# Prompt attention of a decoder step: two heads at once on the two halves of TensorE, and a rearranged opening

## The reference, cut to what matters

```python
s = einsum('bkgqd,bknd->bkgqn', qi, k_cmp) - slopes * d_c      # 32 compressed blocks
p_c = where(ok_c, softmax(where(ok_c, s, NEG_INF)), 0.0)
s = einsum('bkgqd,bkqsd->bkgqs', qi, kg) - slopes * d_s        # selected blocks: at 512 tokens all of them
p_s = softmax(where(d_s >= 0, s, NEG_INF))
s = einsum('bkgqd,bskd->bkgqs', qi, kw) - slopes * d_w         # window, 512 wide: all earlier tokens
p_w = softmax(where(ok_w, s, NEG_INF))
return gi[..., 0:1] * o_c + gi[..., 1:2] * o_s + gi[..., 2:3] * o_w
```

## Time and profile before

| what | value |
|---|---|
| median of 3 runs | 3051.97 us (3050.62 to 3070.57) |
| the profiled execution's own time | 3049.01 us |
| its span | 3047.4 us |
| PE busy, PEld busy | 2885.9 us (95%), 2580.9 us (85%) |
| DVE, ACT, POOL busy | 1246.3 us (41%), 793.8 us (26%), 174.6 us (6%) |
| granted TensorE clock, mean | 0.947 |

### The profile page before, as it was taken

How to read it: one execution, slowest core, us unless ns; L and a number is a source line. 1 busy time by engine, 2 the same in 40 slices (tenths; PEclk the granted TensorE clock), 3 DMA queues, 4 the chain that set the end, 5 groups by cost and what they waited for, 6 DMA issues and landing times. The chain is left out here.

```text
span 3047.4 us, 56435 instructions
## 1 busy us (share of the span) xinstructions
PE 2885.9 (95%) x24825; PEld 2580.9 (85%) x24825; DVE 1246.3 (41%) x1997; ACT 793.8 (26%) x1382; POOL 174.6 (6%) x176
## 2 busy tenths in 40 slices
PE   6999979997999899999998989999999999999997
PEld 6999966777999547999997659999976667999997
DVE  4333355275333342433342023333546663433335
ACT  3222212232222101321220023212326652322222
POOL 1000000001111200000003000000023100000000
PEclk9999989999998558999998999999989997999999
DMA  5222210110000001322226312222221000222222
GB/s 213 93 84 85 76 62 15 69 62 24 4 3 3 32 28 46 134 82 98 83 69 167 126 52 93 76 95 82 96 94 60 1 1 15 86 95 75 94 78 72
DMA packets 36517, 214.80 MB, mean 70 GB/s; under 512 B 5200, under 2 KB 5328, under 8 KB 20336
## 3 DMA queue, kind: packets, MB, share of 16 engines
q1 hardware_dynamic: 27648, 174.34, 16.3%
q0 software_dynamic: 8720, 38.27, 4.2%
HBM read 202.49 MB, written 12.17 MB: 70 GB/s over the span
## 5 line engine op out<-in xcount | busy, mean ns | idle before, releaser
L484 PE MATMUL banks<-xh,wh 128*128 128x272 f32 x3072 | 638.9, 289 | 41.4 <-DVE wl L1435 29.0
L484 PE MATMUL banks<-xh,wl 128*128 128x272 f32 x3072 | 637.5, 289 | 0.0
L484 PE MATMUL banks<-xl,wh 128*128 128x272 f32 x3072 | 635.3, 288 | 0.0
L484 PEld LDWEIGHTS banks<-xh,wh 128*128 128x128 f32 x3072 | 485.7, 189 | 42.2 <-issue 36.4
L484 PEld LDWEIGHTS banks<-xl,wh 128*128 128x128 f32 x3072 | 484.9, 189 | 0.0
L484 PEld LDWEIGHTS banks<-xh,wl 128*128 128x128 f32 x3072 | 481.5, 190 | 0.0
L1435 DVE TENSOR_TENSOR wl<-raw,wh 128x2048 fp32r<-128x2048 f32 (+2 forms) x160 | 323.8, 2024 | 105.7 <-ACT wh L1095 105.7
L1095 ACT ACTIVATE wh<-raw 128x2048 fp32r<-128x2048 f32 (+2 forms) x160 | 270.5, 1691 | 257.9 <-PE banks L484 243.9
L484 PE MATMUL banks<-hh,wl 128*128 128x272 f32 x1408 | 291.4, 288 | 0.0
L484 PE MATMUL banks<-hh,wh 128*128 128x272 f32 x1408 | 291.1, 288 | 0.0
L484 PE MATMUL banks<-hl,wh 128*128 128x272 f32 x1408 | 290.3, 288 | 0.0
(11 more groups left out here) (292 smaller groups left out, 3135.1 us busy)
## 6 DMA issues: line engine op xcount, KB each, us to landing
raw<-in_w_in SPq DMA_DIRECT2D x88, 1024.0 KB, 4.8
raw<-in_w_out SPq DMA_DIRECT2D x32, 768.0 KB, 4.2
raw<-in_w_out SPq DMA_DIRECT2D x32, 640.0 KB, 3.8
raw<-in_w_rk SPq DMA_DIRECT2D x8, 1024.0 KB, 4.8
arena<-in_pages_c POOLq DMA_DIRECT2D x32, 256.0 KB, 7.4
raw<-in_w_kv SPq DMA_DIRECT2D x6, 1024.0 KB, 5.0
raw<-in_w_v SPq DMA_DIRECT2D x4, 1024.0 KB, 4.8
raw<-in_w_o SPq DMA_DIRECT2D x4, 1024.0 KB, 4.8
```

What stands on the lines that cost most here:

```text
L484: ins = mm(pst[:, bank + half, 0:HALF], wt[:, s, w], a[:, half * HALF:(half + 1) * HALF], start=first, stop=last)
```

## The change

Attention works in 32 steps S of a pair of heads (`i = S // 4`, both `p`) and one query tile (`qt = S % 4`).

- `scores(S, k)` does the selected (k = 0) and window keys (k = 1) for both heads, on row halves 0 to 63 and 64 to 127 of the array, into banks 2p+k. The compressed scores of both are one K = 128 product with `kbd`, a block-diagonal copy of the compressed keys (64 columns, bank 4).
- `values(S)` does one query tile for both heads, alternating the two column halves of the array (output rows 0 to 63 and 64 to 127 of bank 5).
- Turned blocks form groups that alternate banks 6 and 7: for qt 0 and 1 one group of both branches for each head, for qt 2 and 3 two groups for each head, and last one for the compressed block of both: 3 or 5 groups a step. `turns_to(S)` counts the groups ahead of step S. Group n waits until group n-2 has been copied.
- The score buffers are six, three steps deep. The maxima, sums and factors of a step lie in `stats`, so reciprocal, gate product and negation are one instruction a step each. The slope goes into the fused instruction as a scalar; q is scaled by 1/(8 slope) instead, through `cbias`. GpSimd's 16 bias instructions go. `kbd` and `vcmp_p` take three more ScalarE copies in the key/value stage.
- GpSimd loads one sample page a step, after `fac_ready` of that step, the sample gates after step 16, and the window values `vwin_c` after the last.
- `raw[:, 1]` serves as a score buffer, so SP loads the first weights of slot 1 of `bo` only when the groups ahead of step 30 have been turned.
- Opening: `x` in four parts; `params` ahead of `const`, with its own semaphore; ScalarE does all `high` first, with the split of the first slot after the fourth, and the squares after; VectorE in the same way; GpSimd holds the LoRA weights and window copies back until both weight slots have landed twice. Only the norm's sum and what follows wait for `const`.

The core of the diff, in its added lines with context (what they replace stands in the kernel above):

```diff
+            for part in range(4):
+                sp.dma_start(hT[:, 2 * part:2 * part + 2], I["x"][:, 2 * part:2 * part + 2])\
+                    .then_inc(x_in[part], 16)
...
+            stream_split("bo", I["w_bo"], free=lambda: sp.wait_ge(turned, turns_to(PAIRS - 2)))
...
+            def scores(S, k):
+                i, qt = S // 4, S % 4
                 nk = P * (qt + 1)
+                if S:
+                    pe.wait_ge(score_taken, 6 * (S - 1) + 2 * (k + 1))
+                for p in range(2):
+                    f = slice(64 * p, 64 * p + 64)
+                    last = mm(pst[:, 2 * p + k, 0:nk], qT[f, i, qt * P:(qt + 1) * P],
+                              (kslc, kwin)[k][f, i // 4, 0:nk], start=True, stop=True)
+                last.then_inc(score_mm, 1)
...
+            def turn_group(n, blocks):
+                if n >= 2:
+                    pe.wait_ge(turn_taken, n - 1)
...
+            def turn_probs(S, p):
+                qt, n = S % 4, turns_to(S)
+                s = sbuf[(2 * S + p) % 6]
+                pe.wait_ge(p_ready, 2 * S + p + 1)
+                slc = [(s[:, x * P:(x + 1) * P], P) for x in range(qt + 1)]
+                win = [(s[:, 512 + x * P:512 + (x + 1) * P], P) for x in range(qt + 1)]
+                if qt < 2:
+                    turn_group(n + p, slc + win)
                 else:
+                    turn_group(n + 2 * p, slc)
+                    turn_group(n + 2 * p + 1, win)
...
+            def values(S):
+                i, qt = S // 4, S % 4
+                pe.wait_ge(turn_taken, turns_to(S + 1))
+                if qt == 0 and i:
+                    pe.wait_ge(o_taken, i)
+                pt = ptS[S % 2]
+                c = [slice((2 * (i // 4) + p) * 64, (2 * (i // 4) + p) * 64 + 64) for p in range(2)]
+                out = [pst[64 * p:64 * p + 64, 5, qt * P:(qt + 1) * P] for p in range(2)]
+                mm(out[0], vcmp_p[0:32, c[0]], ptc[0:32, S % 2, :], start=True, stop=False, skip_group_check=True)
                 for n, v in enumerate((v_slc, v_win)):
+                    for x in range(qt + 1):
+                        for p in (1, 0):
+                            mm(out[p], v[:, x, c[p]], pt[p][:, 512 * n + P * x:512 * n + P * x + P],
+                               start=(p == 1 and n == 0 and x == 0), stop=(p == 0 and n == 1 and x == qt),
+                               skip_group_check=True)
+                mm(out[1], vcmp_p[32:64, c[1]], ptc[32:64, S % 2, :], start=False, stop=True, skip_group_check=True)\
                     .then_inc(o_mm, 1)
...
+            for S in range(PAIRS + 4):
+                live, turning = S < PAIRS, 3 <= S < PAIRS + 3
+                if turning:
+                    turn_probs(S - 3, 0)
+                if live:
+                    scores(S, 0)
+                if turning:
+                    turn_probs(S - 3, 1)
+                if live:
+                    scores(S, 1)
+                    scores_cmp(S)
+                if turning:
+                    turn_cmp(S - 3)
+                if S == PAIRS:
                     sample_scores(0)
+                if S >= 4:
+                    values(S - 4)
...
+            act.wait_ge(params_in, 16)
+            act.wait_ge(eps_set, 3)
             for ft in range(DT):
+                if ft % 2 == 0:
+                    act.wait_ge(x_in[ft // 2], 16)
+                high(Q_G00, ft, xh)
+                if ft == 3:
+                    split("inA0", 0, 0)
+            for ft in range(DT):
                 act.wait_ge(acc_step, ft)
                 act.activation(sg[:, ft % 2, :], hT[:, ft, :], ACT.Square).then_inc(sq_done, 1)
+            act.wait_ge(const_in, 16)
...
+            def exps(S):
+                nk, x = P * (S % 4 + 1), S % 3
+                act.wait_ge(negmax, S + 1)
+                for p in range(2):
+                    s = sbuf[(2 * S + p) % 6]
+                    for n, ap in enumerate((cmpb[:, x, 32 * p:32 * p + 32], s[:, 0:nk], s[:, 512:512 + nk])):
+                        ins = act.activation(ap, ap, ACT.Exp, bias=stats[:, x, 1, 3 * p + n:3 * p + n + 1],
+                                             accum_out=stats[:, x, 2, 3 * p + n:3 * p + n + 1])
+                ins.then_inc(exp_done, 1)
+            def copies(S):
+                qt, n, pt = S % 4, turns_to(S), ptS[S % 2]
+                nk = P * (qt + 1)
+                if S >= 2:
+                    act.wait_ge(o_mm, S - 1)
+                for p in range(2):
+                    if qt < 2:
+                        act.wait_ge(turned, n + 1)
+                        act.activation(pt[p].rearrange("p (k c) -> p k c", k=2)[:, :, 0:nk],
+                                       pst[:, 6 + n % 2, 0:2 * nk].rearrange("p (k c) -> p k c", k=2), ACT.Copy)\
+                            .then_inc(turn_taken, 1)
+                        n += 1
+                    else:
+                        for k in range(2):
+                            act.wait_ge(turned, n + 1)
+                            act.activation(pt[p][:, 512 * k:512 * k + nk], pst[:, 6 + n % 2, 0:nk], ACT.Copy)\
+                                .then_inc(turn_taken, 1)
+                            n += 1
+                act.wait_ge(turned, n + 1)
+                act.activation(ptc[:, S % 2, :], pst[0:64, 6 + n % 2, 0:P], ACT.Copy).then_inc(turn_taken, 1)
+            for S in range(PAIRS + 3):
+                if S >= 3:
+                    copies(S - 3)
+                if S < PAIRS:
+                    exps(S)
...
+            dve.wait_ge(params_in, 16)
             dve.memset(eps[:, 0:1], RMS_EPS).then_inc(eps_set, 1)
             dve.memset(eps[:, 1:2], GN_EPS).then_inc(eps_set, 1)
+            dve.memset(kbd[:], 0.0).then_inc(eps_set, 1)
             clear(0)
             do(dve.tensor_scalar(const[:, C_PAR + 21 * 8:C_PAR + 22 * 8],
                                  const[:, C_PAR + Q_KA * 8:C_PAR + Q_KA * 8 + 8], -1.0, 1.0, ALU.mult, ALU.add))
             for ft in range(DT):
                 low(0, Q_G00, ft, xh, xl)
+                if ft == 3:
+                    split("inA0", 0, 0)
+            for ft in range(DT):
                 sum_square(0, ft, ft % 2)
+            dve.wait_ge(const_in, 16)
...
+            def maxes(S, k):
+                i, qt, x = S // 4, S % 4, S % 3
                 nk = P * (qt + 1)
+                dve.wait_ge(score_mm, 3 * S + k + 1)
+                if k == 0 and S >= 3:
+                    dve.wait_ge(turned, turns_to(S - 2))
+                for p in range(2):
+                    s = sbuf[(2 * S + p) % 6]
+                    n, out, src, t = ((1, s[:, 0:nk], pst[:, 2 * p, 0:nk], (3 - qt) * P),
+                                      (2, s[:, 512:512 + nk], pst[:, 2 * p + 1, 0:nk], (3 - qt) * P),
+                                      (0, cmpb[:, x, 32 * p:32 * p + 32], pst[:, 4, 32 * p:32 * p + 32],
+                                       512 + qt * NCMP))[k]
+                    w = NCMP if k == 2 else nk
+                    dve.tensor_tensor_reduce(out, src, att[:, t:t + w], SLOPES[head_of(i, p)], -3e38, ALU.add,
+                                             ALU.max, stats[:, x, 0, 3 * p + n:3 * p + n + 1])\
+                       .then_inc(score_taken, 1)
+            def negate(S):
+                dve.wait_ge(score_taken, 6 * S + 6)
+                dve.tensor_scalar(stats[:, S % 3, 1, :], stats[:, S % 3, 0, :], -1.0, None, ALU.mult)\
+                   .then_inc(negmax, 1)
+            def factors(S):
+                i, qt, x = S // 4, S % 4, S % 3
+                gates = g_p[:, qt, :].rearrange("q (k g c) -> q k g c", k=4, g=4)[:, 2 * (i // 4):2 * (i // 4) + 2, i % 4, :]
+                dve.wait_ge(exp_done, S + 1)
+                do(dve.reciprocal(stats[:, x, 3, :], stats[:, x, 2, :]))
                 own.wait()
+                fac = stats[:, x, 4, :].rearrange("q (p c) -> q p c", p=2)
+                dve.tensor_tensor(fac, stats[:, x, 3, :].rearrange("q (p c) -> q p c", p=2), gates, ALU.mult)\
+                   .then_inc(fac_ready, 1)
+                dve.wait_ge(fac_ready, S + 1)
+                c = cmpb[:, x, :].rearrange("q (p c) -> q p c", p=2)
+                for p in range(2):
+                    s, nk = sbuf[(2 * S + p) % 6], P * (qt + 1)
+                    for n, w in ((1, slice(0, nk)), (2, slice(512, 512 + nk))):
+                        ins = dve.tensor_scalar(s[:, w], s[:, w], stats[:, x, 4, 3 * p + n:3 * p + n + 1], None,
+                                                ALU.mult)
+                    ins.then_inc(p_ready, 1)
+                dve.tensor_tensor(c, c, fac[:, :, 0:1].to_broadcast([P, 2, NCMP]), ALU.mult).then_inc(cmp_ready, 1)
+            def take_out(i):
+                dve.wait_ge(o_mm, 4 * (i + 1))
+                dve.tensor_copy(oT[:, i, 0:SEQ], pst[:, 5, :]).then_inc(o_taken, 1)
+            for S in range(PAIRS + 1):
+                if S >= 8 and S % 4 == 0:
+                    take_out(S // 4 - 2)
```

(24 more changed lines are left out.)

310 lines of the change are left out of this document (91 added, 219 removed).

## The result

| | before | after |
|---|---|---|
| median, same chip | 3059.93 us (4 runs) | 3092.07 us (3088.53 to 3114.99, 4 runs) |
| the profiled execution | 3049.01 us, span 3047.4 | 3092.99 us, span 3091.3 |
| mean granted clock | 0.947 | 0.919 |

The ratio on record, taken over the executions of both kernels, is 1.0134, 95% interval 1.0093 to 1.0175: slower by 1.3%. The two medians by themselves stand 32 us apart, a ratio of 1.0105, also inside the interval; the fourth execution of the kernel before, 3067.89 us, had moved its median from 3051.97 to 3059.93. First the page of the changed kernel: busy time by engine, the clock in 40 slices of 77 us, and the chain that ended last.

What follows compares the result with a forecast made beforehand. TensorE was taken to bound nearly the whole run before, a chain through the queues attention after. 3049.0 + 39.9 (attention) + 5 (tail) - 10.5 (opening) + 0.7 (copies) = 3084, median 3 us above: 3087 us, range 3058 to 3110.

Steps and rivals of the forecast that it cites:

- The line: Prompt attention: exponentials, first copies, turns, maxima, factors and negation form one chain with nothing beside it, 35.6 us a pair at full clock.
- D: Attention: delay from the end of exps(S-1) until turn_cmp(S-3) is seen, 8.5 us a pair at full clock.
- Its terms: Attention chain, a pair: exponentials 11.1 us, VectorE 15.4, hand-overs 0.6, delay 8.5 at full clock.
- the mixed case: Attention: qt 1 at the low clock, qt 2 at the full, 37.3 us a pair; chance 0.50.
- The clock: Attention: TensorE's idle time each step lowers its clock to 1.2 GHz, stretching a pair from 35.6 to 37.3 us.
- Low throughout: Rival in attention: the chain with the clock low throughout, 39.3 us a pair, 3108 us; chance 0.13.
- TensorE's own work: Attention: TensorE's instructions for a pair of heads take 21 us in place of 30.6, row halves assumed to overlap.
- Attention: From first scores to last negation: 283.9 us against 244.0, +39.9.
- The opening: Kernel start: TensorE starts at 17.6 us, 11.4 earlier; the first norm's sum waits about 1 us: -10.5.
- The tail: From last negation to the samples' first turns: 20.5 to 25 us against 16.0, +5 (4 to 9).
- TensorE's busy share: Sign in the attention trace: the share should fall from 97 to near 60%.
- The rival of the other side: Attention: turning done in time, steps overlap, 26 us a pair, 3007 us; chance 0.07.

Runs made afterwards that it cites:

- the run with the later wait: Changed kernel, first maxima waiting only for probability groups of three steps before, the wait for turned compressed scores put before the maxima overwriting them: 3047.99 us, ratio 0.9981.
- the scaling taken out alone: Changed kernel, VectorE computing all maxima and the negation of a step before scaling the probabilities of the step before: 3034.11 us, ratio 0.9937.
- The smaller filler: Changed kernel plus products of no use where TensorE idles: 8 with qt 3, 2 with qt 0, 2 with qt 1; 3084.34 us, ratio 1.0074.
- the run with VectorE's two edits: Changed kernel, compressed-scores wait moved to the maxima overwriting them, and all maxima ahead of the scaling of the step before: 2986.75 us, ratio 0.9775.
- the turning moved alone: Changed kernel, TensorE issuing a step's scores first, turning, its copies and values one step sooner, VectorE's order kept: 3035.60 us, ratio 0.9948.
- the order by head: Kernel with turning one step earlier and maxima ahead of scaling, scores and values done one head after the other: 3015.58 us, ratio 0.9838.

## Why the prediction was right

The time, 3087 against a measured 3092.07, lies in its range, and by its main step: the new wait closes one line of exponentials, copies, turns, maxima and scaling. That it is only 5 us off is in part luck. The sum on the profiled execution was 3084 against 3093, 8.9 short: attention was 0.7 over, the opening with the new copies 3.9 short (-9.8 against -5.9), the tail 3.7, and 1.9 behind it stood in no term. To this sum came 3 us for the median of the kernel before, while the median after lies 0.9 below its profiled execution.

- **The line.** That `maxes(S, 0)` waits for `turn_cmp(S-3)`, and that for ScalarE's copies behind `exps(S-1)`, is what the rows show 29 times, and what the run with the later wait confirms: 7.0 us a pair came back, where D and the first maxima were the only things it touched. The edits also add up as they should in one line: 45.8 us for the wait alone, 57.1 for the scaling taken out alone, 101.1 for both.
- **Its terms.** Exponentials 11.2 us a pair by the steps of the trace (2.16, 2.59, 3.02, 3.44) against 11.1; VectorE with its hand-overs 37.6 - 11.2 - 10.7 = 15.7 against 16.0; D 10.7 in the later pairs (4.3, 4.2, 0.9, 1.3 for qt 1, 2, 3, 0) against 10.2 in the mixed case (4.3, 3.45, 1.1, 1.3). A pair took 36.7 and later 37.5 against 37.3.
- **The clock.** Low at qt 1, full at qt 2, was the choice, and in the first pairs it is what happened (9.7 and 9.9 us); in the later ones part of the step with qt 2 was low too (10.8). In the first pairs D with qt 2 is about 0.9 us shorter than in the later ones, so the forecast pair, 37.3, lies between the two kinds (36.7 and 37.5) rather than being either. The smaller filler showed both levels of both steps: all full makes 8.15 + 9.92 + 8.81 + 8.12 = 35.0 a pair, all low 9.69 + 11.50 + 8.94 + 8.25 = 38.4 (the 8.94 from an early step with qt 3 of the changed kernel), against 35.6 and 39.3 in the text. Low throughout, the pair would have been 0.9 to 1.7 us longer than it was. The page of the Trainium skill that has the low clock as the default (TensorE: Matmul & The Clock Gate, What's actually happening) agrees with the trace as far as TensorE goes back to it in every pair.
- **TensorE's own work.** 21 us a pair: in the run with VectorE's two edits TensorE is busy 91.22 of 100 us at clock 1.00, times 23.6 is 21.5. The row halves, which no row had shown, overlap as taken: two products of 512 columns in 1.06 us (2418.64 to 2419.70), where the earlier trace rows have one in 0.96.
- **Attention** +39.2 against +39.9.

Four smaller steps were off.

- *The opening*, -10.5: the first product came at 18.55 for 17.6, because the slot's split started at 14.27 for 13 to 13.5. The sum of bytes left out that the second slot's load runs beside the first: by 14.24 us the SP queue had moved 3.79 MB, 0.5 more than `x` and the first slot. The first norm's sums then cost 1.3 us where the text had 1, which makes -9.2. Of this, 3.3 us more were gone at attention's start. 0.7 of it lies at the new copies in the key/value stage, as predicted, about 1.0 between the first norm and 565 us, and 1.3 at the first products of SwiGLU 2. There TensorE has stood idle for 7.1 or 7.2 us in both kernels and starts at the low clock (0.45 us for two instructions that take 0.25 later), until 1803.8 or 6.0 us on after the change, until 1808.4 or 3.3 us on before. The 1.0 goes with a clock of 0.96 in 471 to 557 us where the kernel before has 0.98 in the same work. What makes the low stretch longer in one execution than in the other stays open.
- *The tail*, +5: measured +8.7 (24.8 us against 16.05). The order of its parts was right, but the first sample scores behind the last exponentials ran at the low clock, 7.06 us for the 4.67 of the earlier trace rows. The range of the term, 4 to 9, held it. Behind it another 1.8 were lost, 1.6 of them in the samples, where the clock is 0.71 in 2566 to 2620 and was 0.73 in the same work before.
- *TensorE's busy share* was to fall to near 60%; it fell to 81%. The text divided 21 us of full-clock work by the pair's time and forgot that an instruction at the low clock is busy for longer. The share is the wrong witness where the clock moves; the granted clock beside it, 0.70, pointed to the idle time.
- *The rival of the other side*, "turning done in time", was priced at 26 us a pair and 3007 us. What the runs show for a kernel without the line is 22.6 to 23.6 a pair: the stalls of 2 us that it had were too many, and the scaling needn't stand in the line either. The rule given for when it decides, `turn_cmp(S-3)` before `exps(S-1)` ends, wasn't enough: with the turning moved alone a pair still took 30.7, since the scores then stood behind the turns.

## What to carry to other kernels

When work moves between engines with fixed orders, write the cycle down, from one engine's step to its own next one, and add its terms; the busy shares only give the lower bound. A wait that covers several buffers should be split by who overwrites which: here one count less on the first wait was worth 46 us, and together with the maxima ahead of the scaling 101 us (280.2 to 179.1). In one line each edit gives back its own part, and the parts add. A single one shows about half of what there is: the three single edits stopped at 29 to 32 us a pair, two together gave 23 to 24. And a queue has to be read again after each move: with the turning moved alone VectorE waited for scores instead of turns, and the pair stopped at 30.7.

## What was not expected of the hardware

- Products on different halves overlap also when two of one half come first: four score products in 1.99 us and four value products in 0.66 us in either order. From four value products a head on, the order by head lost most of the overlap (1.58 against 1.09 us for eight products, 3.33 against 1.97 for sixteen).
- A few products in an idle gap raised the mean clock in 2400 to 2500 us from 0.68 to 0.88 without a like gain, since the low stretch moved to the next step and cost up to 1.6 us there. The gaps that the clock fell after were short: from 2300 us to the last negation of the changed kernel TensorE never stood idle for longer than 2.93 us at a time, and its clock was 0.70 in 2400 to 2500.
- The same instructions ahead of attention ended at different times in different executions: the first negation came at 2244.7 us in one kernel with the new opening and at 2270.4 in another; between 720 and 1100 us the granted clock was 0.84 in the first and 0.80 in the second. The changed kernel itself had its first negation at 2261.6 in one execution and at 2270.4 in another. Differences of a few microseconds between kernels are better read from a stage's own length than from the totals.
